# Weight tiles of the 272-token phases placed at other distances, modulo 256 bytes, from the moving tiles

## What is computed

```python
def first_block(...):
    h = jnp.concatenate([meta_b, x], axis=1)                  # 16 + 256 = 272 tokens
    for l in range(DEPTH):
        h = h + 0.5 * swiglu(rmsnorm(h, ffn1_norm[l]), ...)   # (silu(x @ w_gate) * (x @ w_up)) @ w_down
        h = h + hybrid_mixer(rmsnorm(h, mix_norm[l]), ...)
        h = h + 0.5 * swiglu(rmsnorm(h, ffn2_norm[l]), ...)
    return rmsnorm(h, final_norm)[:, N_META:]
```

## Time and profile before

| | |
|---|---|
| time, median of 3 runs | 2178.9 us |
| the profiled execution's own time | 2179.06 us |
| its span, first to last instruction | 2177.3 us |
| TensorE matmul busy (PE) | 2165.6 us, 99% |
| weight loads busy (PEld) | 2148.3 us, 99% |
| VectorE busy (DVE) | 1602.3 us, 74% |
| ScalarE busy (ACT) | 1277.6 us, 59% |
| granted TensorE clock | 1.000 |

### The profile page before, as it was taken

How to read it: one execution, slowest core, us unless ns; L and a number is a source line. 1 busy time by engine, 2 the same in 40 slices (tenths; PEclk the granted TensorE clock), 3 DMA queues, 4 the chain that set the end, 5 groups by cost and what they waited for, 6 DMA issues and landing times.

```text
span 2177.3 us, 49024 instructions
## 1 busy us (share of the span) xinstructions
PE 2165.6 (99%) x18136; PEld 2148.3 (99%) x18136; DVE 1602.3 (74%) x2450; ACT 1277.6 (59%) x1988; POOL 283.1 (13%) x328
## 2 busy tenths in 40 slices
PE   8999999999999999999999999999999999999999
PEld 8999999999999999999999999999999999999999
DVE  6655998665566579888768867988768866786875
ACT  6444786544444368866546646876556635565662
POOL 0001661100100136220020011010010010101000
DMA  6555535556455554455556655356656655446664
GB/s 232 175 190 168 163 118 174 174 174 197 153 179 185 182 164 141 149 189 193 193 178 199 207 179 169 118 185 192 201 180 196 218 162 183 156 156 200 194 213 126
DMA packets 100408, 386.68 MB, mean 178 GB/s; under 512 B 11312, under 2 KB 12464, under 8 KB 100304
## 3 DMA queue, kind: packets, MB, share of 16 engines
q1 hardware_dynamic: 99648, 383.89, 54.8%
q0 software_dynamic: 368, 1.26, 0.2%
q10 hardware_dynamic: 288, 0.12, 0.0%
HBM read 384.18 MB, written 1.05 MB: 177 GB/s over the span
## 4 chain that ended last, share of the span: by engine, by line
PE 97%; DVE 2%; ACT 1%; issue 0%; DMA 0%; ACTq 0%
PE bank L407 30%; PE bank L415 15%; PE bank L414 15%; PE bank L422 14%; PE bank L423 14%; PE bank L785 1%; PE bank L1075 1%; PE bank L1076 1%; PE bank L1077 1%; DVE wlo L438 1%; PE bank L1122 0%; PE bank L735 0%; PE bank L766 0%; PE bank L966 0%; PE bank L969 0%; PE bank L968 0%
## 5 line engine op out<-in xcount | busy, mean ns | idle before, releaser
L407 PE MATMUL bank<-u,whi 128*128 128x256 f32 (+2 forms) x3776 | 1065.7, 282 | 7.2 <-DVE u L476 7.2
L438 DVE TENSOR_TENSOR wlo<-raw,whi 128x1024 fp32r<-128x1024 f32 (+1 forms) x677 | 893.9, 1323 | 176.4 <-ACT whi L431 164.4
L431 ACT ACTIVATE whi<-raw 128x1024 fp32r<-128x1024 f32 (+1 forms) x677 | 746.1, 1113 | 151.0 <-PE bank L415 106.4
L407 PEld LDWEIGHTS bank<-u,whi 128*128 128x128 f32 x3776 | 710.6, 188 | 8.5 <-DVE wlo L438 7.4
L415 PE MATMUL bank<-u,wlo 128*128 128x272 f32 (+1 forms) x1888 | 541.3, 287 | 0.0
L414 PE MATMUL bank<-u,whi 128*128 128x272 f32 (+1 forms) x1888 | 536.5, 284 | 0.0
L422 PE MATMUL bank<-u,whi 128*128 128x256 f32 x1888 | 522.7, 277 | 0.0
L423 PE MATMUL bank<-u,wlo 128*128 128x256 f32 x1888 | 521.4, 276 | 0.0
L407 PE MATMUL bank<-hid,whi 128*128 128x256 f32 (+1 forms) x1408 | 394.2, 280 | 0.0
L415 PEld LDWEIGHTS bank<-u,wlo 128*128 128x128 f32 x1888 | 357.3, 189 | 0.0
L414 PEld LDWEIGHTS bank<-u,whi 128*128 128x128 f32 x1888 | 356.3, 189 | 0.9 <-issue 0.2
(11 more groups left out here) (328 smaller groups left out, 3045.5 us busy)
## 6 DMA issues: line engine op xcount, KB each, us to landing
raw<-w SPq DMA_DIRECT2D x552, 512.0 KB, 3.7
raw<-w SPq DMA_DIRECT2D x128, 704.0 KB, 4.2
h<-xT SPq DMA_DIRECT2D x4, 272.0 KB, 5.8
outT<-h SPq DMA_DIRECT2D x8, 128.0 KB, 4.9
consts<-cst POOLq DMA_DIRECT2D x1, 576.0 KB, 4.8
dist<-cst POOLq DMA_DIRECT2D x1, 192.0 KB, 2.7
rdist<-cst POOLq DMA_DIRECT2D x1, 192.0 KB, 3.1
sgain<-small POOLq DMA_DIRECT2D x1, 145.5 KB, 5.2
```

What stands on the lines that cost most here:

```text
L407: pe.matmul(out[:, cut:cols], w, x[:, cut:cols], start=first, stop=False, skip_group_check=True)
L431: act.activation(weights(0, n), raw[:, n % RING, 0:COLS[n]].rearrange("p (k c) -> p k c", c=128), ACT.Copy).then_inc(hi_ready, 1)
L438: dve.tensor_tensor(weights(1, n), raw[:, n % RING, 0:COLS[n]].rearrange("p (k c) -> p k c", c=128), weights(0, n), ALU.subtract).then_inc ...
```

## The change

It moves operands within their buffers and changes nothing else: no instruction is added or removed, and every access keeps its shape.

```diff
-U_PLACE = {0: (48, 0), 1: (48, 0), 2: (48, 0), 3: (48, 0), 4: (48, 0), ...}
-HID_PLACE = {0: (24, 0), 2: (24, 0), 3: (24, 0), 5: (24, 0), ...}
+U_PLACE = {0: (48, 0), 1: (32, 32), 2: (48, 0), 3: (48, 0), 4: (48, 16), ...}
+HID_PLACE = {0: (24, 16), 2: (24, 32), 3: (24, 48), 5: (24, 0), ...}
...
+FFN_DISTANCES = {0: ((0, 1), (0, 2), (0, 3), (1, 0)), 2: ((2, 0), (2, 1), (2, 3), (3, 0)),
+                 3: ((3, 1), (3, 2), (1.5, 1.5), (0.5, 0.5))}
+GRID = [(p, q) for p in range(4) for q in range(4)]
+MIX_DISTANCES = [(1, 1), *GRID, *(((1, 1),) * 19)]
+AT_PLACE = {y: (1 + (48 - place[0]) // 16) % 4 for y, place in U_PLACE.items()}
+
+def place_of(part, n):
+    y = max(i for i in range(len(PHASES)) if BASE[i]["P"] <= n)
+    j = n - BASE[y]["P"]
+    if COLS[n] != K8 or y > LAST_MIX:
+        return 0
+    if PHASES[y] == "mix":
+        if j >= 36:
+            return META if y == LAST_MIX else 0
+        want = MIX_DISTANCES[j][part]
+    else:
+        want = FFN_DISTANCES[y][j % RING][part]
+    return int(16 * ((want - AT_PLACE[y]) % 4))
...
 def weights(part, n):
-            at = META if BASE[LAST_MIX]["P"] + 36 <= n < BASE[LAST_MIX + 1]["P"] else 0
+            at = place_of(part, n)
```

More of the change, by code:

```diff
@@ L144 @@
 RY_PAD, GAP_STEP, HID_STEP = 144, 144, 320
-U_PLACE = {0: (48, 0), 1: (48, 0), 2: (48, 0), 3: (48, 0), 4: (48, 0), 5: (48, 0), 6: (48, 0), 8: (48, 0), 9: (48, 0), 10: (48, 0), 11: (48, 0), 12: (48, 0), 7: (48, 0)}
-HID_PLACE = {0: (24, 0), 2: (24, 0), 3: (24, 0), 5: (24, 0), 7: (24, 0), 9: (24, 0), 10: (24, 0), 12: (24, 0)}
+U_PLACE = {0: (48, 0), 1: (32, 32), 2: (48, 0), 3: (48, 0), 4: (48, 16), 5: (48, 0), 6: (48, 0), 8: (48, 0), 9: (48, 0), 10: (48, 0), 11: (48, 0), 12: (48, 0), 7: (48, 0)}
+HID_PLACE = {0: (24, 16), 2: (24, 32), 3: (24, 48), 5: (24, 0), 7: (24, 0), 9: (24, 0), 10: (24, 0), 12: (24, 0)}
 CUTS = (0, 252, 128, 0)
 BEHIND_TERMS = [(0, 1), (0, 2), *((t, c) for t in range(1, RT_HEADS + 1) for c in (0, 1)), (RT_HEADS, 5), (RT_HEADS + 1, 0)]
+FFN_DISTANCES = {0: ((0, 1), (0, 2), (0, 3), (1, 0)), 2: ((2, 0), (2, 1), (2, 3), (3, 0)),
[15 more added lines that the diff above has]
+    return int(16 * ((want - AT_PLACE[y]) % 4))
 def build(nc, w8, w11, xT, small, cst, lam, outT):
```

## The result

The changed kernel takes 2185.8 us, the median of 6 runs (2185.5 to 2186.4), against 2178.85 us for the kernel before in the same comparison: a ratio of 1.0033, with an interval of 1.0023 to 1.0043. It is 6.9 us slower, which is more than the 0.2% that a measurement can tell from no change. The forecast was 2182.8 us, 3.9 us slower, in a range of 2172 to 2190. The time lies in the range and the sign is right, but it lies outside "within 0.2%", which I had given the larger chance.

What follows compares the result with a forecast made beforehand. TensorE's row of 18136 matmuls was taken as the bound, their pitch as the time. Terms for distances 0, 3 and 2, 2.9 + 1.6 - 0.6 = 3.9 us, on 2179.06 gave 2183.0, so 2182.8 us as a median; range 2172 to 2190.

Steps and rivals of the forecast that it cites:

- within 0.2%: Whole kernel: time no more than about 4.4 us from no change, which a measurement can't tell apart; chance 0.46.
- What bounds the kernel: Whole kernel: a row of 18136 TensorE matmuls whose pitch is the time; longest wait 7.2 us, once, at the start.
- cover: Gate and up: VectorE, busy 83.29 of 132 us, hides splits even 0.15 us slower; mix phases have less room; nothing added.
- Prices, per slot of a triplet: 272-column loops: each slot pays over distance 1 by its own distance: 2.5 ns at 2, 2.7 at 0, 1.2 at 3.
- kinds with equal slots that differ: Sign in the panels' pitches: if kinds holding the same distances ran differently, slots don't add and the prediction is wrong.
- The sum, term by term: Feed-forward and mix phases: changed slots times price for distances 0, 3 and 2: 2.9 + 1.6 - 0.6 = 3.9 us.
- the half quarters: Two panels in four of phase 3: no row, taken as unchanged, worth -1.6 to 1.8 us at the ends.
- Slower at the full price: Mainly phase 2 and its down projection: distances 0 and 3 both cost 4.1 ns; 9.3 us slower, 2188.3 us; chance 0.36.
- prices near mine: The forecast's own case over all changed loops: 3.9 us slower, 2182.8 us; chance 0.38.
- Faster: 272-column loops leave a bad rhythm, distances 0 and 3 at -2.3 ns: 6.2 us quicker, 2172.7 us; chance 0.18.
- Nothing: 272-column loops: a fixed distance averages out, or the pitch has another cause; 2178.9 us; chance 0.08.
- The ends -2.3 and 4.1: Lowest and highest ns per slot allowed for distances 0 and 3, from phase 4's quick panels against phases 11 and 5.

Runs made afterwards that it cites:

- by the weights: Against the kernel before, weights alone moved so that gate and up, phase 1's panels and phase 4's panels 0 to 19 stand at (3, 3): 2176.6 us.

## Why the prediction was right in sign and too small

**What bounds the kernel** was right: TensorE's row of matmuls sets the end, its pitch is the time, and neither the waits nor the 256-column feed-forwards of phases 5 on moved. No cover was used up: the slower or quicker splits of VectorE and ScalarE show up nowhere. That the pitch comes from where TensorE's two operands lie to each other was right too: moving either alone changes it, by the low parts and by `u` even with all splits writing where they did, and moving both together at (1, 1) leaves it at 372.8 ns. That 256 bytes is the period was assumed without a row; one loop bears it out, with 368.3 ns at 3 and at 3 plus 256 bytes.

**The step that failed is "Prices, per slot of a triplet".** It took a price for each distance and added three of them. The prediction named the sign by which that would be seen, kinds with equal slots that differ: (0,2,1) and (1,0,2) hold the same three distances and run at 375.8 and 377.4 ns. The stronger proof is that one slot moved in the same way, q from 0 to 1, costs 7.1 ns beside p = 3 and gains 4.7 beside p = 0. The pitch belongs to the whole pair, with the loop it stands in, and at (3, 3) even then to one of two rhythms.

**The sum, term by term** (predicted, then measured): phase 0 0.62 and 1.3 us; phase 2 1.0 and 1.15; phase 3 0.47 and 1.8; down 1.1 and 1.75; mix 0.7 and 1.2. All five are too low, and 3.9 became 7.2. Most was missing in phase 3: the half quarters were "taken as unchanged" and cost 2.9 and 7.7 ns a triplet over 88 triplets each, 0.93 us, within the 1.8 us that I had kept as their upper end (with the prediction's own 2.5 ns for distance 2 that end comes to 1.7). Phase 0's first kind, put at 372.6 ns, ran at 375.0, and its fourth, put at 375, at 377.4. Phase 2's (3, 0), with three changed slots put at 376.5, ran at 374.6. The down loops, put at 372.5, 371.0 and 372.3, ran at 373.3 all three.

That the sign came out right was in part luck. The same prices put (3, 3), slots (3,3,0), at 375.0 ns, a cost of 2.6, and by the weights most loops ran it at 368.3, a gain of 4.5. The change happens to hold no such pair in its feed-forwards.

**The rivals.** "Slower at the full price" gave 2188.3 us, "prices near mine" 2182.8; the result lies between. The first had its place in phase 2, whose gate and up cost the least of the three, and its premise that distance 1 is the one good place fell with (3, 3) at 368.3. "Faster" had the right mechanism for another pair: the 272-column loops can leave their rhythm towards a quicker one, but none of the twelve pairs of the change does it. "Nothing" is out. The rule that would have given it, that TensorE's two read ports are independent and never wait (the Trainium skill, "SBUF — State Buffer", "Who interferes with whom"), is not what is seen here: the same matmuls at the same clock take 368.3 to 381.7 ns a triplet when nothing but addresses is moved.

**The chances.** The rows already held the warning: the prediction noted that one and the same distance ran at 113.3 ns in phase 5 and at 117.6 in phase 11 and called it a tight and a loose pattern, and then took constants from differences between such rows. If two rows with equal distances differ by 13 ns a triplet, a price of 2.5 ns taken from two other rows has no firm sign, and the price of a place not yet run could only be bounded. The ends -2.3 and 4.1 were of the right kind; the spread seen in gate and up is -4.5 to +8.9 ns a triplet around 372.8.

Left open: why a pair has the pitch it has, which place makes a loop find the quicker of its rhythms, whether other pairs than (3, 3) have two, and the 0.46 us of phase 11. Most pairs were seen in one or two loops, and each pitch comes from one profiled execution of its kernel.

## What to carry to other kernels

Where matmuls run back to back with no wait, the time can still depend on where weights and moving tiles lie modulo 256 bytes, by 2.7% of the pitch in down (370.0 to 380.0 ns), 3.6% in gate and up (368.3 to 381.7) and 5.9% at 256 columns (340.0 to 360.0). Don't add up prices per operand: run the whole loop at each candidate place, judge it by the matmuls in a settled stretch, and look at the mean, as a median hides a pattern of several steps. And a quick place is not yet a quick kernel: what runs just before the loop can throw it into the slower rhythm, so each loop has to be looked at in the final kernel.

## What the runs showed of the hardware that I had not expected

- One loop at fixed addresses, shapes and clock has more than one steady pitch: 368.3 and 375.0 ns a triplet at (3, 3) with 272 columns, in phase 2 of two kernels. At 256 columns and distance 3 two phases of one form ran at 340.0 and 353.3 ns. A pitch holds for up to hundreds of matmuls and changes where other matmuls come in between; two of them switched it from 375.0 to 368.3 in four phases of one kernel and from 368.3 to 375.0 in the fifth.
- The steady pitches lie on a grid: 368.3, 370.0, 371.7, 373.3, 375.0, 378.3, 380.0 and 381.7 ns are 884, 888, 892, 896, 900, 908, 912 and 916 cycles at 2.4 GHz, all multiples of 4; so are 340.0 (816), 353.3 (848) and 360.0 (864) at 256 columns. The pitches off the grid (372.8, 376.0, 377.2 and 379.7) belong to patterns of several triplets, such as 371, 371, 377 with a mean of 372.8.
- Eight bytes can matter: down of phases 2 and 3 runs at 370.0 ns at distance 1, and at 380.0 with `hid` two elements nearer in one and further in the other.
